# One sum in memory for all experts in place of an even and an odd one, in a two-layer hybrid backbone with a mixture of experts

## The chip, the cores and the metric

The kernel runs on one core of a Trainium2 chip, in one launch. The metric is the device time of that core in microseconds (us). Lower is better.

## What is computed

The reference is a two-layer backbone over 256 latent tokens and 256 context tokens of width 1024 (float32). Each layer has a mixer (state-space, gated-recurrence and delta-rule head groups) and then a mixture of 64 experts, of which every token uses 8. The change is in the second part:

```python
def _routed_experts(h, router_w, router_bias, w_gate, w_up, w_down):
    scores = jax.nn.sigmoid(h @ router_w)
    _, idx = lax.top_k(scores + router_bias, TOP_K)
    gate = ...
    ...
    def expert_block(args):
        xb, e = args
        return (jax.nn.silu(xb @ w_gate[e]) * (xb @ w_up[e])) @ w_down[e]
    ...
    return jnp.zeros_like(h).at[token].add(contrib)

def _moe(...):
    ...
    return routed + shared
...
h = h + g_f * _moe(...)
```

Layer 0 routes 512 tokens (4096 pairs of token and expert), layer 1 only the 256 latent tokens (2048 pairs). A shared expert, which every token uses, is added.

## The kernel before

Each engine (matrix, vector or DVE, scalar or ACT, Pool, and SP, which issues plain transfers) has its own instruction stream, written by hand, and they meet at semaphores. `S[name]` is a semaphore; `wait(name, n, l)` waits for its n-th count in layer `l`. A DMA adds 16 to its semaphore when it has landed.

After the mixer the token rows are stored to the array `ffn_rows` in memory, each with its 64 gates behind it. For each expert the list of its tokens (`idx_in`) comes out of a small matmul. An expert has one block of up to 128 rows; where it has at most 64 tokens all work is done on 64 ("narrow"), else on 128 ("wide"). The flag for this is `more`, which each engine loads from on-chip memory and branches on (`by_count` on Pool, L740 to L748). Rows of the list past the expert's last token point outside the array and are skipped.

The loop over experts runs in four slots `s` (expert e = 4i + s). Its work by engine:

- SP loads the 3 MB of weights of an expert (L531, L532 gate and up, L536 down), up to four experts ahead, as slots come free.
- Pool issues for expert e first `gather` for e+3 (L737: rows of `ffn_rows` into `xg[s]`, which stands in `featT` or `R`), once the matrix engine has read the slot; then it waits for both halves of expert e's scaled result (`oe_act`, `oe_dve`, L759 to L761) and for an earlier scatter (L763 to L765), and issues the scatter of e (L768): each row of `oe[s % 2]` is added to its token's row in memory by the DMA itself (`compute_op=ALU.add`). `pool_step` holds this.
- The matrix engine's step of e (`pe_step`) is: turn e's hidden values; gate and up projection of e+1 (128x256 matmuls); transpose the gathered rows of e+2 (L1743, waiting for the gather); down projection of e (128x512 matmuls).
- DVE and ACT scale half of e's result each with the token's gate into `oe[s % 2]` (L1665, L1056). Before that they wait for the scatter of e-2, which read the same buffer (L1658, L1051).

There are two sums in memory. Scatters of even experts add to `acc_dram` (`ffn_sum_even`), which is first filled with the shared expert's output (L551). Those of odd experts add to `acc_odd` (`ffn_sum_odd`), which SP fills with zeros from the tile `zero` during the input projections (L503 to L505). Two scatters that add to one array must not be in flight together, since both may touch the same token's row. So a scatter waits for the one of e-2, the last on its array.

After the last scatter SP reads both sums back (L601, L602) into `yraw` (which is `featT`) and `sums` (in `R`), and DVE does for each live tile of 128 tokens: add the two, multiply by the gate of the residual, add to `h` (L1711 to L1715). The live tiles are four in layer 0 and two in layer 1.

Of the kernel before, what the change touches and what calls it, by code (L numbers as in the profile page):

```python
# [8 lines left out]
F32 = mybir.dt.float32  # L9
I32 = mybir.dt.int32  # L10
U32 = mybir.dt.uint32
BF16 = mybir.dt.bfloat16
ALU = mybir.AluOpType
# [3 lines left out]
P = 128  # L17
DEPTH = 2
DM = 1024
# [130 lines left out]
def build(nc, A, out, scratch):  # L150
    f_dram, acc_dram, acc_odd = scratch
    with ExitStack() as ctx:
# [187 lines left out]
        for name, n in (  # L340
# [28 lines left out]
            ("sh_ps", 2), ("sh_silu", 1), ("sh_mul", 1), ("shd_ps", NT), ("shd_sb", NT), ("acc_zeroed", 16 * NT),  # L369
# [4 lines left out]
            ("sums_loaded", 32), ("gf_ps", 1),  # L374
# [12 lines left out]
        def tk(c):  # L387
            return slice(c * P, (c + 1) * P)
# [20 lines left out]
        def _(sp):  # L409
# [77 lines left out]
            for l in range(DEPTH):  # L487
# [15 lines left out]
                for c in live:  # L503
                    sp.dma_start(acc_odd[tk(c), :].rearrange("p (a b) -> p a b", b=32),
                                 zero[:, :].unsqueeze(1).to_broadcast([P, DM // 32, 32])).then_inc(S["acc_zeroed"], 16)  # L505
# [95 lines left out]
                sp.dma_start(yraw[:, rows, :], acc_odd.rearrange("(c p) f -> p c f", p=P)[:, rows]).then_inc(S["sums_loaded"], 16)  # L601
# [10 lines left out]
        def _(pool):  # L612
            G = nc.gpsimd

            def wait(name, n, l):
                pool.wait_ge(S[name], l * PER[name] + n)
                pool.sem_inc(S["past"], 1)
# [35 lines left out]
            for l in range(DEPTH):  # L653
# [96 lines left out]
                def pool_step(i, s, ahead):  # L750
# [12 lines left out]
                    if not (first and s < 2):  # L763
                        pool.wait_ge(S[f"scattered{s % 2}"], l * (8 * NE) + i * 32 + (s // 2) * 16)
                        pool.sem_inc(S["past"], 1)  # L765

                    def rows(n):
                        pool.indirect_dma_start((acc_dram, acc_odd)[s % 2], bass.IndirectOffsetOnAxis(idxS[s][0:n, 0:1].bitcast(U32), 0),  # L768
                                                oe[s % 2][0:n, :], None, bounds_check=TOK - 1, oob_is_err=False,
                                                compute_op=ALU.add).then_inc(S[f"scattered{s % 2}"], 16)  # L770
# [5 lines left out]
                wait("acc_zeroed", 16 * nl, l)  # L776
# [313 lines left out]
        def _(dve):  # L1090
# [92 lines left out]
            for l in range(DEPTH):  # L1183
# [527 lines left out]
                wait("sums_loaded", 16 + 32, l)  # L1711
                for c in live:
                    tt(sums[:, c, :], sums[:, c, :], yraw[:, c, :], ALU.add)
                    tt(sums[:, c, :], sums[:, c, :], bank(2 * (c // 2), 2), ALU.mult)
                    tt(h[:, c, :], h[:, c, :], sums[:, c, :], ALU.add)  # L1715
# [620 lines left out]
```

## Time and profile before

| what | us |
|---|---|
| median of 3 runs | 2808.56 |
| the runs | 2806.84 to 2814.77 |
| the profiled execution, its own time | 2818.87 |
| span of its trace | 2817.2 |
| matrix engine busy | 2371.4 (84%) |
| DVE busy | 1365.4 (48%) |
| ACT busy | 730.4 (26%) |
| Pool busy | 608.4 (22%) |

The profile is of one execution. Busy is the time in which an engine had an instruction running; transfers are told by queue: q1 is that of the plain transfers of SP, q0 that of the gathers and scatters of Pool. The experts' loop of layer 0 stands in the trace from 865 to 1524 us, that of layer 1 from 2207 to 2783 us. In the timeline an issue row such as `POOL L768 DMA_INDIRECT` lasts as long as Pool takes to write the transfer's list, not until the data have landed.

### The profile page before, as it was taken

To read this page: it belongs to the slowest core of one execution; us is meant where nothing else is said; L and a number is where in the kernel's file an instruction comes from. 1 tells how busy PE (TensorE), PEld (TensorE's weight loads), DVE (VectorE), ACT (ScalarE), POOL (GpSimd) and SP (SyncE) were. 2 spreads that over 40 slices of the span, in tenths; PEclk is the share of its full clock that TensorE was granted. 3 is DMA by queue.
4 is the path that set the end of the run, shared out by engine and by line. 5 is a ranking of instruction groups with operands and counts; after the bars stand their busy time and mean duration, and the time that the engine had idled before them with its cause. 6 is when DMAs were issued, how large, how long until landed. Compare 5 with 4: busy or idle time off the path is not lost.

```text
span 2817.2 us, 47122 instructions
## 1 busy us (share of the span) xinstructions
PE 2371.4 (84%) x15388; PEld 1547.9 (55%) x15389; DVE 1365.4 (48%) x2960; ACT 730.4 (26%) x1274; POOL 608.4 (22%) x640
## 2 busy tenths in 40 slices
PE   5999888886788989898996698888877888888884
PEld 2347788885644545454553245788866444444442
DVE  4433487875334444444432543367853444444443
ACT  2116333231112222222221114533221222222221
POOL 0000354450002222222221000135320122222221
PEclk9999899997889999999998799999989999999887
DMA  6643100001538999999995252200017899999993
GB/s 259 246 172 77 18 2 1 1 1 39 207 120 313 369 361 348 347 352 333 362 328 172 94 204 70 54 1 1 1 35 273 318 366 369 375 357 362 366 364 116
DMA packets 187925, 574.33 MB, mean 204 GB/s; under 512 B 55742, under 2 KB 99078, under 8 KB 148870
## 3 DMA queue, kind: packets, MB, share of 16 engines
q1 hardware_dynamic: 162950, 520.48, 49.9%
q0 software_dynamic: 24832, 51.97, 7.9%
q8 instruction: 86, 1.41, 0.2%
q14 instruction: 57, 0.47, 0.1%
HBM read 554.89 MB, written 53.15 MB: 216 GB/s over the span
## 4 chain that ended last, share of the span: by engine, by line
PE 52%; DMA 17%; DVE 14%; issue 6%; ACT 4%; DVEq 3%; POOLq 2%; ACTq 1%; SPq 0%; POOL 0%
PE ps L1739 47%; DMA featT<-ffn_rows,idx_in 11%; PE ps L1743 5%; DVE R L1102 3%; DMA R<-ffn_rows,idx_in 3%; DMA R<-in_exp_up 2%; ACT R L832 2%; DVEq L1099 2%; DVE featT L1102 2%; POOLq L744 1%; DVE R L1665 1%; DVE ring L1102 1%; DVE R L1376 1%; ACT L832 1%; DMA R<-ffn_sum_even 1%
## 5 line engine op out<-in xcount | busy, mean ns | idle before, releaser
L1739 PE MATMUL ps<-R 128*64 128x256 f32 (+6 forms) x9312 | 1263.7, 393 | 81.5 <-issue 25.3
L1739 PEld LDWEIGHTS ps<-R 128*64 128x64 f32 (+2 forms) x9312 | 752.2, 156 | 456.8 <-issue 236.5
L832 ACT ACTIVATE R<-ps 128x256 f32<-128x256 f32 (+3 forms) x395 | 175.5, 444 | 984.2 <-PE ps L1739 926.4
L1739 PE MATMUL ps<-featT,ring 128*128 128x512 f32 (+1 forms) x768 | 318.9, 573 | 0.3 <-issue 0.3
L1102 DVE TENSOR_TENSOR R<-R,ps 128x256 f32<-128x256 f32 (+2 forms) x250 | 143.7, 575 | 361.2 <-ACT R L832 232.3
L1665 DVE TENSOR_SCALAR R<-ps,idx_out 64x512 f32<-64x512 f32 x256 | 193.2, 755 | 170.7 <-PE ps L1739 168.8
L1739 PE MATMUL ps<-ring,R 128*128 128x128 f32 (+2 forms) x1200 | 243.9, 335 | 17.2 <-DVE ring L1102 8.4
L1111 DVE COPY R<-ps 128x512 f32<-128x512 f32 (+2 forms) x280 | 153.8, 549 | 212.6 <-PE ps L1743 181.0
L1056 ACT ACTIVATE R<-ps,idx_out 64x512 f32<-64x512 f32 x256 | 174.6, 682 | 280.6 <-PE ps L1739 279.0
L1739 PEld LDWEIGHTS ps<-featT,ring 128*128 128x128 f32 x768 | 150.6, 200 | 164.4 <-issue 158.5
L1743 PE MATMUL ps<-ident,featT 128*128 128x128 f32 x864 | 134.4, 306 | 126.5 <-DMA featT<-ffn_rows,idx_in 91.6
L1739 PEld LDWEIGHTS ps<-ring,R 128*128 128x128 f32 x1200 | 193.7, 198 | 49.5 <-issue 29.9
L669 POOL TENSOR_TENSOR R<-ring,lev 128x512 f32<-128x512 f32 x56 | 72.6, 1297 | 623.2 <-DVEq L1338 307.1
L768 POOL DMA_INDIRECT ffn_sum_even<-R,idx_out x64 | 94.9, 1483 | 495.6 <-DVE idx_in L1102 361.0
L1743 PEld LDWEIGHTS ps<-ident,featT 128*128 128x128 f32 x864 | 106.1, 155 | 169.8 <-DMA featT<-ffn_rows,idx_in 112.4
L768 POOL DMA_INDIRECT ffn_sum_odd<-R,idx_out x64 | 95.9, 1498 | 424.1 <-issue 290.1
L1036 ACT ACTIVATE R<-ps 128x512 f32<-128x512 f32 x128 | 76.6, 599 | 278.0 <-PE ps L1743 275.2
L737 POOL DMA_INDIRECT featT<-ffn_rows,idx_in x96 | 95.1, 990 | 245.1 <-issue 245.1
L1743 PE MATMUL ps<-ident,R 128*128 128x128 f32 x616 | 106.3, 290 | 26.0 <-DMA R<-ffn_rows,idx_in 23.7
L1739 PE MATMUL ps<-ring,featT 128*128 128x256 f32 x512 | 113.8, 383 | 1.0 <-issue 1.0
L1739 PEld LDWEIGHTS ps<-ring,featT 128*128 128x128 f32 x512 | 97.8, 192 | 17.1 <-issue 4.0
L669 POOL TENSOR_TENSOR R<-R,lev 128x512 f32<-128x512 f32 x56 | 72.9, 1302 | 116.5 <-PE ps L1739 89.1
(201 smaller groups left out, 1981.0 us busy)
## 6 DMA issues: line engine op xcount, KB each, us to landing
R<-in_exp_gate SPq DMA_DIRECT2D x128, 1024.0 KB
R<-in_exp_up SPq DMA_DIRECT2D x128, 1024.0 KB
R<-in_exp_down SPq DMA_DIRECT2D x128, 1024.0 KB
R<-in_w_mod SPq DMA_DIRECT2D x48, 1024.0 KB, 7.5
ring<-in_w_in SPq DMA_DIRECT2D x30, 1024.0 KB, 5.3
ring<-in_w_out SPq DMA_DIRECT2D x8, 1024.0 KB, 7.2
ffn_sum_odd<-zero SPq DMA_DIRECT2D x6, 512.0 KB, 11.0
ffn_rows<-X SPq DMA_DIRECT2D x6, 512.0 KB, 9.1
```

Of the source, the lines that this page charges most:

```text
L669: do(G.tensor_tensor(NTm[:, run % 2, :, :], AT[u % 2][:, :, :], lev[:, UNITS[u][1], j, :].unsqueeze(1).to_broadcast([P, HH, P]), ALU.mult) ...
L737: pool.indirect_dma_start(xg[s][0:n, :], None, f_dram, bass.IndirectOffsetOnAxis(idxG[s][0:n, 0:1].bitcast(U32), 0), bounds_check=TOK - 1, ...
L768: pool.indirect_dma_start((acc_dram, acc_odd)[s % 2], bass.IndirectOffsetOnAxis(idxS[s][0:n, 0:1].bitcast(U32), 0), oe[s % 2][0:n, :], Non ...
L832: do(C.activation(out_, in_, func, **kw), name)
L1036: do(C.activation(xgT[b][:, 0:4, :].rearrange("p k t -> p (k t)"), ps[:, 0, :], ACT.Identity), "xt_sb")
L1056: ins = C.activation(oe[s % 2][at_, 0:512], ps[0:HD, 4 + 2 * (s % 2) + u, :], ACT.Identity, scale=idxS[s][at_, 1:2])
L1099: dve.drain()
L1102: do(V.tensor_tensor(out_, a, b, op), name)
L1111: do(V.tensor_copy(out_, in_), name)
L1665: ins = V.tensor_scalar(oe[s % 2][at_, 512:DM], ps[HD:P, 4 + 2 * (s % 2) + u, :], idxS[s][at_, 1:2], None, ALU.mult)
L1739: return MM(out_, lhsT, rhs, start=start, stop=stop)
L1743: return nc.tensor.transpose(out_, in_, ident[0:k, 0:k])
```

## The change

One array `acc_dram` (`ffn_sum`) takes the scatters of all experts. It is filled with the shared expert's output as before; the array of zeros, its stores and its semaphore are gone. The scatter of e now waits for that of e-1: in slot s for the semaphore of the other parity, with the count that it has when e-1 has landed. Only the very first scatter waits for none. After the loop one array is read back, and DVE's addition of the two sums is gone. The two buffers `oe` and the waits of DVE and ACT for e-2 are as before.

```diff
--- before.py
+++ after.py
@@ -148,7 +148,7 @@
 
 
 def build(nc, A, out, scratch):
-    f_dram, acc_dram, acc_odd = scratch
+    f_dram, acc_dram = scratch
     with ExitStack() as ctx:
         def sb(name, shape, dt=F32):
             return ctx.enter_context(nc.sbuf_tensor(name, shape, dt))
@@ -366,12 +366,12 @@
             ("mask_ready", 1), ("pos_ps", 1), ("w_ready", 1), ("w_stored", 16),
             ("hot_ready", NE + 1), ("slot_ps", NSLOT), ("flag_ready", 1),
 
-            ("sh_ps", 2), ("sh_silu", 1), ("sh_mul", 1), ("shd_ps", NT), ("shd_sb", NT), ("acc_zeroed", 16 * NT),
+            ("sh_ps", 2), ("sh_silu", 1), ("sh_mul", 1), ("shd_ps", NT), ("shd_sb", NT), 
 
             ("w0", 0), ("w1", 0), ("w2", 0), ("w3", 0), ("wd0", 0), ("wd1", 0), ("wd2", 0), ("wd3", 0),
             ("gathered0", 4 * NE), ("gathered1", 4 * NE), ("gathered2", 4 * NE), ("gathered3", 4 * NE), ("xt_ps", NE), ("xt_sb", 2 * NE), ("gu_ps", NE), ("gu_silu", NE), ("gu_mul", NE), ("ht_ps", NE), ("ht_sb", NE),
             ("dn_ps", NE), ("oe_act", NE), ("oe_dve", NE), ("idx_in", NE), ("idx_out", NE), ("scattered0", 8 * NE), ("scattered1", 8 * NE),
-            ("sums_loaded", 32), ("gf_ps", 1),
+            ("sums_loaded", 16), ("gf_ps", 1),
 
             ("ov_w", 48 * OVER), ("ov_hot", OVER), ("ov_ip", OVER), ("ov_tab", OVER), ("ov_g", OVER), ("ov_xt", OVER), ("ov_xs", OVER),
             ("ov_gu", OVER), ("ov_sl", OVER), ("ov_mu", OVER), ("ov_dn", OVER),
@@ -500,9 +500,6 @@
                     if kind == "mod" and q < n_mod:
                         mod_block(at_mod + q)
                         q += 1
-                for c in live:
-                    sp.dma_start(acc_odd[tk(c), :].rearrange("p (a b) -> p a b", b=32),
-                                 zero[:, :].unsqueeze(1).to_broadcast([P, DM // 32, 32])).then_inc(S["acc_zeroed"], 16)
                 sp.dma_start(rw[:, :, :], A["router_w"][L1].rearrange("o (k p) n -> p (o k) n", p=P)).then_inc(S["rw_loaded"], 16)
                 wout = A["w_out"][L1].rearrange("o (k p) n -> p (o k) n", p=P)
 
@@ -598,7 +595,6 @@
                 for b in range(2):
                     wait(f"scattered{b}", 8 * NE, l)
                 rows = slice(live[0], NT)
-                sp.dma_start(yraw[:, rows, :], acc_odd.rearrange("(c p) f -> p c f", p=P)[:, rows]).then_inc(S["sums_loaded"], 16)
                 sp.dma_start(sums[:, rows, :], acc_dram.rearrange("(c p) f -> p c f", p=P)[:, rows]).then_inc(S["sums_loaded"], 16)
             sp.wait_ge(S["h_ready"], DEPTH + 1)
             sp.dma_start(grow[:, 0, :], A["norm_final"].rearrange("(o f) -> o f", o=1).to_broadcast([P, DM])).then_inc(S["head_loaded"], 16)
@@ -760,12 +756,13 @@
                     pool.wait_ge(S["oe_dve"], e + 1)
                     pool.sem_inc(S["past"], 1)
 
-                    if not (first and s < 2):
-                        pool.wait_ge(S[f"scattered{s % 2}"], l * (8 * NE) + i * 32 + (s // 2) * 16)
+
+                    if not (first and s == 0):
+                        pool.wait_ge(S[f"scattered{(s + 1) % 2}"], l * (8 * NE) + i * 32 + ((s + 1) // 2) * 16)
                         pool.sem_inc(S["past"], 1)
 
                     def rows(n):
-                        pool.indirect_dma_start((acc_dram, acc_odd)[s % 2], bass.IndirectOffsetOnAxis(idxS[s][0:n, 0:1].bitcast(U32), 0),
+                        pool.indirect_dma_start(acc_dram, bass.IndirectOffsetOnAxis(idxS[s][0:n, 0:1].bitcast(U32), 0),
                                                 oe[s % 2][0:n, :], None, bounds_check=TOK - 1, oob_is_err=False,
                                                 compute_op=ALU.add).then_inc(S[f"scattered{s % 2}"], 16)
                     by_count(i * NSLOT + s, rows)
@@ -773,7 +770,6 @@
                 for s in range(3):
                     gather(s, s)
 
-                wait("acc_zeroed", 16 * nl, l)
                 for b in range(2):
                     wait(f"x_stored{b}", 16 * nl, l)
                 for s in range(NSLOT):
@@ -1708,9 +1704,8 @@
                         dve.sem_inc(S[name], OVER)
 
                 wait("gf_ps", 1, l)
-                wait("sums_loaded", 16 + 32, l)
+                wait("sums_loaded", 16 + 16, l)
                 for c in live:
-                    tt(sums[:, c, :], sums[:, c, :], yraw[:, c, :], ALU.add)
                     tt(sums[:, c, :], sums[:, c, :], bank(2 * (c // 2), 2), ALU.mult)
                     tt(h[:, c, :], h[:, c, :], sums[:, c, :], ALU.add)
                 dve.drain().then_inc(S["h_ready"], 1)
@@ -2328,8 +2323,7 @@
         A[name] = nc.dram_tensor(f"in_{name}", a.shape, mybir.dt.from_np(a.dtype), kind="ExternalInput").ap()
     out = nc.dram_tensor("out", (1, SEQ, DM), F32, kind="ExternalOutput").ap()
     scratch = (nc.dram_tensor("ffn_rows", (TOK, FROW), F32, kind="Internal").ap(),
-               nc.dram_tensor("ffn_sum_even", (TOK, DM), F32, kind="Internal").ap(),
-               nc.dram_tensor("ffn_sum_odd", (TOK, DM), F32, kind="Internal").ap())
+               nc.dram_tensor("ffn_sum", (TOK, DM), F32, kind="Internal").ap())
     build(nc, A, out, scratch)
     r = run_bass_kernel_spmd(nc, [arrays], core_ids=[0])
     return r.results[0]["out"]
```

The order of Pool, slots 0 and 1 of the loop over experts 4 to 59 (`ffn_sum_even` and `ffn_sum_odd` are the two sums; the two DMA rows of one scatter are its wide and its narrow form). Before:

```order
L759 REGISTER_ALU
L764 REGISTER_ALU [waits oe_act,oe_dve]
L744 ISA [waits scattered0]
L744 TENSOR_LOAD more
...
L768 DMA ffn_sum_even<-R,idx_out 512x1024
...
L734 REGISTER_ALU [waits xt_ps]
L744 ISA [waits idx_in]
...
L737 DMA featT<-ffn_rows,idx_in 64x1088
...
L744 ISA [waits oe_act,oe_dve,scattered1]
...
L768 DMA ffn_sum_odd<-R,idx_out 512x1024
```

And with the change:

```order
L755 REGISTER_ALU
L761 REGISTER_ALU [waits oe_act,oe_dve]
L740 ISA [waits scattered1]
L740 TENSOR_LOAD more
...
L765 DMA ffn_sum<-R,idx_out 512x1024
...
L730 REGISTER_ALU [waits xt_ps]
L740 ISA [waits idx_in]
...
L733 DMA featT<-ffn_rows,idx_in 64x1088
...
L761 REGISTER_ALU [waits oe_act,oe_dve]
L740 ISA [waits scattered0]
...
L765 DMA ffn_sum<-R,idx_out 512x1024
```

The scatter of slot 0 waits for the semaphore of the odd scatters, that of slot 1 for that of the even ones, which is the scatter issued directly before it. The gather between them keeps its place.

The order of DVE after the loop of layer 0 (first tile and the beginning of the second; `R` holds the sum, `featT` the odd sum, `ps` the gate). Before:

```order
L1102 TENSOR_TENSOR R<-R,featT 128x1024 [waits sums_loaded,gf_ps]
L1102 TENSOR_TENSOR R<-R,ps 128x1024
L1102 TENSOR_TENSOR h<-h,R 128x1024
L1102 TENSOR_TENSOR R<-R,featT 128x1024
L1102 TENSOR_TENSOR R<-R,ps 128x1024
```

And with the change:

```order
L1098 TENSOR_TENSOR R<-R,ps 128x1024 [waits sums_loaded,gf_ps]
L1098 TENSOR_TENSOR h<-h,R 128x1024
L1098 TENSOR_TENSOR R<-R,ps 128x1024
```

One of three passes a tile is gone.

## Rows read from the trace of the kernel before

**Rows 1.** The page: the chain that ended last, its share of the span by line.

```profile
PE ps L1739 47%; DMA featT<-ffn_rows,idx_in 11%; PE ps L1743 5%; DVE R L1102 3%; DMA R<-ffn_rows,idx_in 3%; DMA R<-in_exp_up 2%; ACT R L832 2%; DVEq L1099 2%; DVE featT L1102 2%; POOLq L744 1%; DVE R L1665 1%; DVE ring L1102 1%; DVE R L1376
```

**Rows 2.** Windows: us, busy (instructions) by engine, matrix clock, DMA share, GB/s.

```profile
864.70:1524.00 659.30, 597.69 (x4436) 325.23 (x4432) 267.18 (x608) 146.34 (x249) 156.61 (x124) 0.96 0.96 334
2206.90:2783.00 576.10, 491.37 (x3392) 260.61 (x3388) 252.18 (x607) 146.59 (x250) 149.84 (x124) 0.93 0.97 350
269.00:290.00 21.00, 20.74 (x93) 17.26 (x92) 4.01 (x10) 10.72 (x11) 0.00 (x0) 1.00 0.91 149
```

**Rows 3.** Waits in the loops: us in total, times, longest; layer 1, then 0.

```profile
PE ps L1743 <- DMA featT<-ffn_rows,idx_in: 58.7, 25, 4.8
...
PE ps L1743 <- DMA featT<-ffn_rows,idx_in: 32.9, 14, 5.7
```

**Rows 4.** Timeline, Pool: start, us, instruction [idle before]; each loop's first, five between.

```profile
864.66 1.52 POOL L768 DMA_INDIRECT ffn_sum_even<-R,idx_out  x1 [19.15 <-DVE idx_in L1102]
...
2206.89 1.49 POOL L768 DMA_INDIRECT ffn_sum_even<-R,idx_out  x1 [13.69 <-DVE idx_in L1102]
...
2355.46 1.44 POOL L768 DMA_INDIRECT ffn_sum_even<-R,idx_out  x1 [6.85 <-DVE idx_in L1102]
2357.20 0.97 POOL L737 DMA_INDIRECT featT<-ffn_rows,idx_in  x1 [0.30 <-issue]
2362.68 1.44 POOL L768 DMA_INDIRECT ffn_sum_odd<-R,idx_out  x1 [4.51 <-DVE idx_in L1102]
...
2373.61 1.44 POOL L768 DMA_INDIRECT ffn_sum_even<-R,idx_out  x1 [8.21 <-DVE idx_in L1102]
...
2380.38 1.44 POOL L768 DMA_INDIRECT ffn_sum_odd<-R,idx_out  x1 [4.07 <-issue]
```

**Rows 5.** Chain that ended last: start, us, what; from 2357 us.

```profile
2357.20 8.56 DMA featT<-ffn_rows,idx_in
...
2415.19 29.84 DMA R<-in_exp_up
```

**Rows 6.** Last scatters: chain (layer 0 and 1), and timeline of the last in layer 1.

```profile
1523.96 6.09 DMA ffn_sum_odd<-R,idx_out
...
2782.96 4.48 DMA ffn_sum_odd<-R,idx_out
...
2779.79 1.52 DVE L1665 TENSOR_SCALAR R<-ps,idx_out 64x512 f32<-64x512 f32 x2 [4.99 <-PE ps L1739]
```

**Rows 7.** DMA, q0 (packets, MB, share) in 2437.68:2442.2, 2442.2:2443.6, 1388:1391.5.

```profile
q0 software_dynamic: 29, 0.03, 2.4%
q0 software_dynamic: 54, 0.08, 29.3%
...
q0 software_dynamic: 70, 0.21, 27.3%
```

**Rows 8.** Groups by form: down projections of layer 0's loop, then layer 1's.

```profile
L1739 PE MATMUL ps<-R 128*64 128x512 f32 x744 | 187.0, 639 | 4.5 <-DVE R L1111 2.7 <-issue 1.2
...
L1739 PE MATMUL ps<-R 128*64 128x512 f32 x552 | 153.9, 688 | 6.6 <-issue 5.5
```

**Rows 9.** Read-back: timeline (layer 0), chain (layer 1), issues to landing (2048, 1024 KB).

```profile
1532.15 0.39 SPq L601 DMA_DIRECT2D featT<-ffn_sum_odd  x1
...
1545.97 1.23 DVE L1102 TENSOR_TENSOR R<-R,featT 128x1024 f32<-128x1024 f32 x1 [23.55 <-DMA R<-ffn_sum_even]
1547.27 1.22 DVE L1102 TENSOR_TENSOR R<-R,ps 128x1024 f32<-128x1024 f32 x1
...
2789.95 7.00 DMA R<-ffn_sum_even
...
featT<-ffn_sum_odd SPq DMA_DIRECT2D x1, 2048.0 KB, 8.2
...
featT<-ffn_sum_odd SPq DMA_DIRECT2D x1, 1024.0 KB, 4.9
```

**Rows 10.** Timeline, SP: the zero stores of layer 0.

```profile
268.96 15.05 SPq L504 DMA_DIRECT2D ffn_sum_odd<-zero  x4
```

## The prediction

> **What bounds the kernel now.** I read the chain that ended last on the page first [rows 1]: matmuls of one line hold 47% of it, but 11% + 3% are gathers of token rows and 2% are loads of weights. So inside the expert loops a transfer and not arithmetic decides part of the time. The windows of the two loops say how much [rows 2]: 659.3 us for the 64 experts of layer 0 and 576.1 us for layer 1, together 44% of the span. In both the DMA engines are busy (share 0.96 and 0.97), and in layer 1 the matrix engine is busy 491 of 576 us only. The waits name the cause [rows 3]: in layer 1 it sat 58.7 us before transposes (L1743) whose rows came from a gather, in layer 0 32.9 us (and less before those of the slot in `R`).
>
> The timeline of the Pool engine shows why a gather can be late [rows 4]. Pool does everything in one order: scatter of expert e-1, gather for e+3, scatter of e, gather for e+4. A gather is issued 1.74 us after the scatter in front of it (2355.46 and 2357.20), and in the chain it lands 8.56 us later at 2365.76, where the transposes begin [rows 5]. Those are in the matrix engine's step of expert e+1; after them come its down projection, the scaling (L1056, L1665), and the scatter of e+1 at 2373.61. So each second scatter is tied to the one two before it through a gather, and the gaps alternate: 7.2, 10.9, 6.8 us between the four issues shown. Two such ties, of odd and of even experts, run side by side.
>
> **The change, part by part.**
>
> *The wait (slower).* In the order of Pool [the two extracts of Pool's loop in the section on the change] scatter e waited for scatter e-2; now it waits for e-1. Before, that wait was never late: with gaps of 7 to 11 us two of them give 17 us or more. What is queued behind it on Pool is the gather for e+4, and behind that the matrix engine. So the price depends on how long a scatter takes to land, which the trace tells only at the loops' ends, where no weights move: 6.09 us and 4.48 us [rows 6]. Under load I bound it from the DMA queue of Pool. The scatter issued at 2437.68 is followed by 4.5 us in which its queue moves 0.03 MB, then by 1.4 us with 0.08 MB (its rows), then come the bytes of the gather behind it [rows 7]: its data are over 5.9 us after the issue, and the semaphore comes later still. From above, the gather queued behind a scatter lands 1.74 + 8.56 = 10.3 us after that scatter's issue [rows 4, 5]. I take 7.6 us for an expert of up to 64 rows, nearer to the row of the thing itself. For an expert with more rows ("wide") the queue after the issue at 1381.75 is still moving 0.21 MB between 6.25 and 9.75 us [rows 7]; I take 9.9 us. From the landing to the next issue Pool needs the semaphore wait, a value load and a branch; the same path after the scaling takes from 2779.79 + 1.52 = 2781.31 to 2782.96, 1.65 us, say 1.7 [rows 6].
>
> That gives each gap a floor: 9.3 us, and 11.6 us behind a wide expert. The number of wide experts comes from the down projections: 8 matmuls an expert, 16 a wide one, so 744 = 512 + 8 x 29 and 552 = 512 + 8 x 5 [rows 8]; 28 of the 29 have a successor. The floors of the 63 gaps of layer 0 add up to 35 x 9.3 + 28 x 11.6 = 650 us, of layer 1 to 58 x 9.3 + 5 x 11.6 = 597 us. The gaps themselves add up to 659.3 us (864.66 to 1523.96) and 576.1 us (2206.89 to 2782.96) [rows 4, 6]. The floors are only an average, and a gap that is longer for another reason gives nothing back. Laid over the 126 gaps between the 128 issue rows (first and last of each loop in rows 4 and 6), 30 gaps of layer 0 and 36 of layer 1 lie under their floor, by 56 and 80 us in total. How much of this is lost? A short gap that is stretched delays one tie; the long gap behind it is held by the other tie, whose gather was issued before, so it shrinks by as much until the two together reach two floors. I therefore take gaps in pairs, and count only what two floors exceed the measured pair: 22.6 us in layer 0, 35.3 us in layer 1. Sum **+58 us**. Both ends: with 7.0 and 9.2 us for the landing the pairs give 9.8 + 15.8 = +26 us, with 8.0 and 10.3 us 35.1 + 52.0 = +87 us. The slope is steep: half a microsecond of landing time is worth about 30 us.
>
> *One read-back in place of two (faster).* In layer 0 the first of two 2 MB reads is issued at 1532.15, the second behind it, and DVE starts at 1545.97, released by the second; the first alone landed 8.2 us after its issue. With one read left DVE starts at about 1532.15 + 8.2 + 0.1 = 1540.4: -5.5 us. In layer 1 the second is issued at 2789.95 and lands at 2796.95; the first, issued 0.4 us earlier, landed after 4.9, at 2794.4: -2.6 us [rows 9]. All of it lies on the chain.
>
> *The additions (faster).* DVE does three passes for each live tile (sum of the halves, gate, residual), 1.30 us from start to start [rows 9]; the first falls away (the extract of DVE's rows in the section on the change). Four tiles in layer 0 are -5.2 us, two in layer 1 -2.6 us, on the chain, since the passes follow each other without a gap and the next layer starts from their result.
>
> *Zeroing (nothing).* Six stores of zeros go. The four of layer 0 keep the sync queue for 15.05 us from 268.96 on and the DMA engines at 0.91, but the matrix engine is busy 20.74 of those 21.0 us, and the queue has only the router weights behind it before a long wait [rows 2, 10]. They cover nothing and hide under the matmuls.
>
> Sum: +58 - 5.5 - 2.6 - 5.2 - 2.6 = **+42 us**. The profiled execution took 2818.87 us (span 2817.2), 10 us over the median of 2808.56; I put the difference on the median: 2808.6 + 42 = 2851 us.
>
> The trace has the first bytes of a scatter 4.5 us after its issue under load [rows 7], and 4.48 us even for a whole one without load. The Trainium skill, page "DMA: Bandwidth & Descriptors", section "Anatomy of one DMA — SWDGE (gpsimd) path", gives a DMA issued by GpSimd about 2.0 us plus its bytes at 436 GB/s, which for 64 rows of 4 KB would be an estimated 2.6 us. By that the wait would cost nothing, and the sum would be the -16 us of the other terms; the trace does not agree.
>
> **The rivals.**
>
> *The landing is covered (faster).* If a scatter, now alone on its array and never beside another scatter, lands as at the loops' ends (4.5 to 6.1 us), the floor is 6.2 to 7.8 us, under nearly every gap (the shortest is 6.0), and the pairs lose under 1 us. Then only the savings remain: 2808.6 - 16 = 2793 us. It decides from a landing under about 6.5 us. For: rows 6. Against: rows 7, where the queue is shared with the weights in every loop step, since DMA is busy 96%. The skill's rule above would also end here. Chance 0.07.
>
> *The weights hold the loop (no change).* The chain has stretches of 29.84 us in which a weight load and not a gather is waited for [rows 5], and layer 1 moves 350 GB/s. If the weights set the pace, a late scatter is absorbed wherever they are late too, and only the floors' own excess remains: nothing in layer 0 and 597 - 576 = 21 us in layer 1, so 2808.6 + 21 - 16 = 2814 us, inside 0.3%. Against: most pieces of layer 1's chain are gathers. Chance 0.09.
>
> *Nothing is absorbed (much slower).* If both ties are tight, each stretched gap is lost in full: 56 + 80 = 136 us, 2808.6 + 136 - 16 = 2929 us. Against: the long gap has a matrix-engine wait in it (58.7 us in 25 waits, 2.3 us each [rows 3]), which can shrink. Chance 0.08.
>
> *The wait does not hold Pool* (its count is reached already, so the change is the read-back alone) would look like the first rival; the counts in the two extracts speak against it. It is in that chance.
>
> **How the numbers follow.** The forecast, loops slower by 26 to 87 us and the ends faster by 16, has the other 0.76: 2819 to 2880 us, likeliest 2851. The range goes somewhat beyond on both sides, half way into "nothing is absorbed" and to the edge of "weights hold the loop": 2814 to 2892. About 0.3%, 8 us, is what a measurement of this kernel can tell from no change. Slower: all of the forecast but its lowest edge and the third rival, 0.83. Same: the second rival and that edge, 0.10. Faster: 0.07.
>
> **What would show it.** In the changed profile: the gaps between scatter issues hardly under 9 us and no longer alternating; loops of about 682 and 611 us; Pool idle before a scatter until the DMA of the one in front; DVE's first pass starting some 8 us after the read is issued in layer 0; two passes a tile. It is wrong if gaps of 7 us survive (the landing is short) or if loop times stay while the gaps level out (everything absorbed).

## The result, and the profile after

The changed kernel takes 2858.53 us (median of 4 runs, 2845.71 to 2861.67) against 2808.95 us (4 runs) for the kernel before: ratio 1.0165, 95% interval 1.013 to 1.0199. It is slower by 49.6 us in the medians, by 37 to 56 us within the interval; 42 us and 2851 us were forecast, with a range of 2814 to 2892 us. The profiled execution took 2861.67 us (span 2859.9), 42.7 us over the span of before.

The page has the chain that ended last by line. It answers to [rows 1]:

```profile
PE 43%; DMA 27%; DVE 14%; issue 6%; ACT 3%; POOLq 3%; DVEq 2%; ACTq 1%; POOL 0%; SPq 0%
PE ps L1734 40%; DMA ffn_sum<-R,idx_out 19%; DMA featT<-ffn_rows,idx_in 5%; PE ps L1738 3%; DVE R L1098 3%; ACT R L828 2%; POOLq L740 2%; DMA R<-ffn_rows,idx_in 2%; DVE featT L1098 2%; DVEq L1095 1%; DVE ring L1098 1%; DVE R L1372 1%; ACT L
```

A scatter's landing was hardly in the chain before; now it holds 19% of the span, and the gathers fell from 14% to 7%. The windows of the two loops, first scatter to last, in the columns of [rows 2]:

```profile
864.50:1561.60 697.10, 613.77 (x4438) 330.42 (x4434) 267.25 (x608) 146.14 (x249) 156.00 (x124) 0.94 0.92 316
2230.40:2831.40 601.00, 499.16 (x3395) 263.55 (x3392) 251.30 (x607) 147.39 (x250) 150.01 (x124) 0.92 0.94 336
```

Layer 0's loop grew from 659.3 to 697.1 us, layer 1's from 576.1 to 600.9 us, together by 62.7 us, and the DMA engines are less busy (0.92 and 0.94 against 0.96 and 0.97). The rest went the other way: between the loops 682.9 us became 668.8, and after the last scatter 34.2 became 28.5. That is -19.8 us, and with -0.1 before the first scatter the sum is the 42.7 us.

The waits of the matrix engine for gathers in the stretches of layer 0 and layer 1, as in [rows 3] (us in total, times, longest):

```profile
PE ps L1738 <- DMA featT<-ffn_rows,idx_in: 57.3, 22, 6.8
PE ps L1738 <- DMA R<-ffn_rows,idx_in: 17.6, 6, 5.9
...
PE ps L1738 <- DMA featT<-ffn_rows,idx_in: 74.7, 32, 6.2
PE ps L1738 <- DMA R<-ffn_rows,idx_in: 14.1, 10, 3.9
```

They rose from 52.7 to 74.9 us in layer 0 and from 62.6 to 88.8 us in layer 1. The matrix engine was also busy for longer with the same instructions: in layer 0 613.77 us at a mean granted clock of 0.94, where it had been 597.69 us at 0.96, and in layer 1 499.16 us at 0.92, where it had been 491.37 us at 0.93 [rows 2]. The timeline of Pool in layer 1, near the place of [rows 4]:

```profile
2380.57 1.44 POOL L765 DMA_INDIRECT ffn_sum<-R,idx_out  x1 [7.04 <-issue]
2382.53 0.96 POOL L733 DMA_INDIRECT R<-ffn_rows,idx_in  x1 [0.53 <-issue]
2391.03 1.44 POOL L765 DMA_INDIRECT ffn_sum<-R,idx_out  x1 [7.54 <-issue]
...
2401.11 1.44 POOL L765 DMA_INDIRECT ffn_sum<-R,idx_out  x1 [7.37 <-issue]
...
2410.34 1.44 POOL L765 DMA_INDIRECT ffn_sum<-R,idx_out  x1 [6.52 <-issue]
```

These are the 16th to the 19th scatter of the layer, and the gaps are 10.5, 10.1 and 9.2 us. In the kernel before the same three gaps were 9.8, 7.2 and 10.9 us (the four issues of [rows 4] are the 17th to the 20th). The short gap grew by 2.9 us, and the long one behind it shrank by 1.7 us only. The chain in the same stretch shows what sets them (start, us, what):

```profile
2380.57 8.79 DMA ffn_sum<-R,idx_out
2389.53 0.29 POOLq L740
2389.86 0.15 POOLq L740
...
2391.03 8.41 DMA ffn_sum<-R,idx_out
...
2401.11 7.57 DMA ffn_sum<-R,idx_out
```

A scatter lands after 8.79 us, Pool loads the flag and branches, and 1.67 us after the landing the next scatter leaves. That repeats without a matmul in between. In layer 0 the chain changes between the two kinds of cause:

```profile
1125.51 11.80 DMA ffn_sum<-R,idx_out
...
1138.87 10.37 DMA ffn_sum<-R,idx_out
...
1150.91 7.60 DMA ffn_sum<-R,idx_out
...
1162.03 11.50 DMA R<-ffn_rows,idx_in
1173.57 1.97 PE ps L1738 x8
```

Three landings in a row, then a gather that was queued behind the scatter of 1160.01 and holds the transposes at 1173.57. The ends, from the chain, answer to [rows 6] and [rows 9]:

```profile
1561.60 5.91 DMA ffn_sum<-R,idx_out
...
1569.60 7.72 DMA R<-ffn_sum
1577.42 1.22 DVE R L1098
1578.71 1.22 DVE h L1098
1580.01 1.22 DVE R L1098
...
2831.35 4.41 DMA ffn_sum<-R,idx_out
...
2837.82 4.78 DMA R<-ffn_sum
2842.69 1.22 DVE R L1098
```

One read of 2 MB holds DVE for 7.8 us, where two held it for 13.8; two passes a tile are left.

### The profile page after: what moved, and what is told of

The parts are those of the page before. It is cut to its first block, busy times and chain, and to the rows that moved or that the text cites. A ratio compares the mean times of both kernels' runs of the same rounds, so it can differ in the third digit from the quotient of the medians.

```text
span 2859.9 us, 47130 instructions
## 1 busy us (share of the span) xinstructions
PE 2388.9 (84%) x15388; PEld 1551.0 (54%) x15389; DVE 1353.7 (47%) x2954; ACT 729.6 (26%) x1274; POOL 607.7 (21%) x640
## 4 chain that ended last, share of the span: by engine, by line
PE 43%; DMA 27%; DVE 14%; issue 6%; ACT 3%; POOLq 3%; DVEq 2%; ACTq 1%; POOL 0%; SPq 0%
PE ps L1734 40%; DMA ffn_sum<-R,idx_out 19%; DMA featT<-ffn_rows,idx_in 5%; PE ps L1738 3%; DVE R L1098 3%; ACT R L828 2%; POOLq L740 2%; DMA R<-ffn_rows,idx_in 2%; DVE featT L1098 2%; DVEq L1095 1%; DVE ring L1098 1%; DVE R L1372 1%; ACT L828 1%; DMA ring<-in_sh_down 1%; DVE R L1661 1%
## 5 line engine op out<-in xcount | busy, mean ns | idle before, releaser
L1734 PE MATMUL ps<-R 128*64 128x256 f32 (+6 forms) x9312 | 1278.9, 397 | 72.8 <-DVEq L1377 19.2
L765 POOL DMA_INDIRECT ffn_sum<-R,idx_out x128 | 190.6, 1489 | 983.5 <-issue 796.1
L1734 PE MATMUL ps<-featT,ring 128*128 128x512 f32 (+1 forms) x768 | 313.1, 564 | 0.3 <-issue 0.3
L1738 PE MATMUL ps<-ident,featT 128*128 128x128 f32 x864 | 141.6, 317 | 165.8 <-DMA featT<-ffn_rows,idx_in 131.9
L1738 PEld LDWEIGHTS ps<-ident,featT 128*128 128x128 f32 x864 | 111.9, 161 | 210.0 <-DMA featT<-ffn_rows,idx_in 158.5
L1738 PEld LDWEIGHTS ps<-ident,R 128*128 128x128 f32 x616 | 67.0, 145 | 55.9 <-DMA R<-ffn_rows,idx_in 39.5
## 6 DMA issues: line engine op xcount, KB each, us to landing
R<-in_exp_up SPq DMA_DIRECT2D x128, 1024.0 KB, 10.4
```

What stands on the lines that cost most here:

```text
L765: pool.indirect_dma_start(acc_dram, bass.IndirectOffsetOnAxis(idxS[s][0:n, 0:1].bitcast(U32), 0), oe[s % 2][0:n, :], None, bounds_check=TO ...
L1734: return MM(out_, lhsT, rhs, start=start, stop=stop)
L1738: return nc.tensor.transpose(out_, in_, ident[0:k, 0:k])
```

## The experiments

The theory to be tested is that the whole loss is the new wait, which sets a floor under each gap between scatters (landing plus 1.7 us) and also holds the gather that stands behind the scatter in Pool's order. The rivals in what follows are that one array is dearer by itself, that the loss is the floor alone or the gather alone, and that the weights hold the loop.

"Loops" below are the times from the first to the last of a layer's 64 scatter issues in the profiled execution. "Landing" is the mean over these 64, from the issue to the last of the scatter's semaphore counts in the trace. (In the trace of the kernel before, 34 of the 128 scatters lack some of their 16 counts; the last one recorded stands for them.) Both are of one execution each. Ratios are to the kernel before on the same chip, with their 95% interval; its own medians beside the experiments were 2812.7 us (e1 to e4), 2812.0 us (e5 to e8), 2810.2 us (e9 to e11) and 2813.7 us (e12).

| kernel | median, us | ratio | loops, us | landing, us |
|---|---|---|---|---|
| before | 2808.95 | 1 | 659.3, 576.1 | 8.9, 7.8 |
| the change | 2858.53 | 1.0165 (1.013 to 1.0199) | 697.1, 600.9 | 8.1, 7.5 |
| e1 the wait alone | 2875.9 | 1.0223 (1.0191 to 1.0254) | 693.6, 601.4 | 8.0, 7.5 |
| e2 the ends alone | 2793.73 | 0.9937 (0.9919 to 0.9955) | 658.5, 573.8 | 8.8, 7.8 |
| e3 before, early gather | 2804.44 | 0.9965 (0.9947 to 0.9984) | 648.1, 575.2 | 9.0, 7.9 |
| e4 change, early gather | 2810.79 | 0.9991 (0.9977 to 1.0005) | 662.2, 590.1 | 8.8, 7.7 |
| e5 before, less traffic | 2775.05 | 0.9867 (0.9852 to 0.9882) | 632.4, 562.0 | 7.4, 7.4 |
| e6 change, less traffic | 2789.19 | 0.9915 (0.9896 to 0.9933) | 663.4, 559.1 | 7.3, 6.7 |
| e7 change, zero stores kept | 2850.04 | 1.0124 (1.0105 to 1.0143) | 683.6, 606.4 | 8.2, 7.5 |
| e8 two sums, early gather and read | 2802.36 | 0.9965 (0.9952 to 0.9979) | 647.6, 575.8 | 9.2, 7.9 |
| e9 change, swapped | 2804.88 | 0.9985 (0.9972 to 0.9998) | 658.9, 579.0 | 8.8, 7.5 |
| e10 before, swapped | 2789.85 | 0.9932 (0.9915 to 0.9948) | 646.6, 567.2 | 9.7, 8.1 |
| e11 change, early, less traffic | 2669.08 | 0.9515 (0.9471 to 0.9559) | 598.5, 508.3 | 7.6, 6.3 |
| e12 before, early, less traffic | 2620.98 | 0.9314 (0.9295 to 0.9332) | 587.6, 459.0 | 8.0, 7.6 |

**The wait alone.** Kernel before, with

```diff
-                    if not (first and s < 2):
-                        pool.wait_ge(S[f"scattered{s % 2}"], l * (8 * NE) + i * 32 + (s // 2) * 16)
+                    if not (first and s == 0):
+                        pool.wait_ge(S[f"scattered{(s + 1) % 2}"], l * (8 * NE) + i * 32 + ((s + 1) // 2) * 16)
```

> The kernel before with both sums, zero stores, read-backs and additions kept; only the wait of each scatter is changed from the one of e-2 to the one of e-1. Theory (the wait costs the loops, the ends give back): both loops as long as in the changed kernel, 63 gaps of about 697 us in layer 0 and 601 us in layer 1, together 55 to 65 us more than before, stretches outside the loops as before; time about 2809 + 62 = 2871 us. Rival (one array in place of two is dearer by itself, because every scatter now adds to rows that the one in front of it has just written): the loops grow by under 20 us here, time under 2830 us.

Measured: 2875.9 us, +63 us on the median of before beside it (2812.7). The loops took 693.6 and 601.4 us, +59.6 us, as in the changed kernel within 4 us. One array instead of two adds nothing that can be seen; the rival falls.

**The ends alone.** The zero stores, the read of the odd sum and the addition taken out of the kernel before:

```diff
-                sp.dma_start(yraw[:, rows, :], acc_odd.rearrange("(c p) f -> p c f", p=P)[:, rows]).then_inc(S["sums_loaded"], 16)
...
-                    tt(sums[:, c, :], sums[:, c, :], yraw[:, c, :], ALU.add)
```

> The kernel before without the zero stores, the read-back of the odd sum and DVE's addition; what the odd experts contribute is left out of the result. Waits of the scatters as before. Theory: loops as before (659 and 576 us for the 63 gaps), ends shorter by 10.7 us after layer 0 and 5.2 us after layer 1, time about 2809 - 16 = 2793 us; if the changed kernel's 14 us between the loops are all of this part, 2789 us. Rival (the ends are hidden or given back by a later start of something else): within 5 us of before.

Measured: 2793.73 us, -0.63%, which is -18 us. This version leaves the odd experts out of the result, and layer 1 has six wide experts by it where there were five. The loops stayed (-0.8 and -2.3 us). Between the loops it was 669.1 us (-13.8), at the end 28.6 us (-5.6). The two halves add up: a ratio of 1.0223 and one of 0.9937 make 1.0159, against 1.0165 measured for both together.

**The gather out of the way.** Pool's step issues the gather of e+4 where it issued that of e+3, one expert earlier, so that it stands in front of the wait and not behind it:

```diff
-                    if ahead > 3:
-                        if not (first and s == 0):
-                            pool.wait_ge(S["xt_ps"], e)
-                            pool.sem_inc(S["past"], 1)
-                        gather((s + 3) % NSLOT, i * NSLOT + s + 3)
+                    if ahead > 4:
+                        pool.wait_ge(S["xt_ps"], e + 1)
+                        pool.sem_inc(S["past"], 1)
+                        gather(s, i * NSLOT + s + 4)
...
-                for s in range(3):
+                for s in range(4):
                     gather(s, s)
```

> The kernel before with Pool's order changed: the gather of expert e+4 is issued before the scatter of e and not behind it, as soon as the matrix engine has turned e's rows and the list of e+4 is there; a fourth gather is issued before the loop. Two sums and the wait for e-2 stay. Theory (scatters are tied two by two through a gather queued behind them): the matrix engine's waits for gathers (120 us in both loops) nearly vanish, and the loops fall to what matmuls or weights allow: layer 0 about 600 to 620 us, layer 1 about 550 to 570 us, time 2750 to 2775 us. Rival (the gathers are late because the DMA engines are full): the gather only lands as late as before, loops within 10 us of before, time above 2795 us.

> The changed kernel with the same early gather. Theory (with the wait for e-1 each gap has a floor of landing + 1.7 us, whatever the gather does): the loops stay at the sum of the floors, about 660 to 690 us and 590 to 600 us, so the time falls by 5 to 40 us only, to 2820 to 2850 us, and Pool waits for the scatter in front before nearly every scatter. Rival (the wait costs only because it holds the gather behind it): with the gather in front of it the cost vanishes, the loops come within 15 us of those of the kernel before with the early gather, time under 2790 us.

Both gave part of an answer. In e3 the matrix engine's waits for gathers vanished, as the theory said (no such row is left in either loop), but the time fell by 8 us only, outside what it forecast. The waits of layer 0 and layer 1 and the chain say where it went:

```profile
PE ps L1738 <- issue: 47.3, 24, 6.4
...
PE ps L1738 <- issue: 85.3, 44, 6.1
...
2313.01 28.53 DMA R<-in_exp_up
2341.54 1.21 issue
2342.75 3.70 PE ps L1738 x32
```

The matrix engine now stops before the gate and up projection, and the chain runs through a load of up weights that takes 28.5 us from its issue. The kernel before was close to this second bound: layer 1's loop did not get shorter at all (575.2 against 576.1 us). In layer 1's loop loads of up weights hold 30% of e3's chain, in layer 0's 20%. So in layer 1 gathers that came late by 63 us in total cost nearly nothing, because the weights were as late. The rival of e3 was right on the time, and not in its reason: the gathers take as long to land as before (9.5 and 7.9 us on the mean, after 9.6 and 8.0), but they come in time.

In e4 the cost of the wait is then what a floor costs. The chain through it:

```profile
1218.75 7.09 DMA ffn_sum<-R,idx_out
...
1227.53 8.46 DMA ffn_sum<-R,idx_out
...
1237.59 10.01 DMA ffn_sum<-R,idx_out
...
1249.20 10.36 DMA ffn_sum<-R,idx_out
```

All 126 gaps of e4 are the landing plus 1.45 to 1.71 us: the loops are the floor itself. They are 14.1 and 14.9 us longer than in e3, 29 us together. The time came out at 2811 us, under the 2820 us that the theory set as its lower edge and far above the rival's 2790. Against the changed kernel the loops are 35 and 11 us shorter. So of the wait's 62.7 us 29 us are the floor. The gather held behind it takes 45.7 us, less the 12.1 us that the same place of the gather had cost in the kernel before (659.3 - 648.1 and 576.1 - 575.2), which is 34 us. These are differences of single executions; e7 below shows by how much such loops differ.

**The same without a head start.** In e4 the gather also left earlier. Here gather and scatter only change places behind the scaling:

```diff
                     pool.wait_ge(S["oe_act"], e + 1)
                     pool.wait_ge(S["oe_dve"], e + 1)
                     pool.sem_inc(S["past"], 1)
+                    if ahead > 4:
+                        pool.wait_ge(S["xt_ps"], e + 1)
+                        pool.sem_inc(S["past"], 1)
+                        gather(s, i * NSLOT + s + 4)
```

and the gather of e+3 at the head of the step is gone.

> The changed kernel with gather and scatter swapped behind the scaling: once expert e is scaled, Pool issues the gather of e+4 first, and only then waits for the scatter of e-1 and issues the scatter of e. The gather so starts at the point where it would in a loop without the new wait, no earlier than the scaling as in e4. Theory (of the 62 us that the wait costs, the larger part is the gather held behind it, and 29 us are the floor of landing plus restart): loops near those of e4 (662 and 590 us), at most 10 us longer each, time 2808 to 2828 us. Rival (e4 was faster because its gathers start some 5 us ahead of the scaling, not because they are out of the wait): loops near those of the changed kernel (690 to 697 and 595 to 601 us), time above 2840 us.

> The same swap in the kernel before, with its two sums and the wait for e-2: the partner of e9. Theory (before the change nothing late stands in front of the gather, so the swap only starts it 1.7 us earlier): between the kernel before and e3, 2800 to 2812 us, loops 650 to 659 us and 575 us. Then e9 is slower than this one by the floor alone: 29 us in the loops, 10 to 15 us in the time. Rival (scatters that leave 1.3 us later cost by themselves): slower than before.

Measured: e9 2804.88 us, under the range expected, with loops of 658.9 and 579.0 us. So the order alone does it, and the rival falls: the changed kernel with its two issues swapped is no slower than the kernel before. Here too each of the 126 gaps is the landing plus 1.45 to 1.71 us. e10 took 2789.85 us, 10 us under the lower edge of what was expected, and is the fastest of the versions that compute the whole result: -0.68% against the kernel before (0.9915 to 0.9948), -2.3% against the changed one (0.9932 over 1.0165). Its waits for gathers, in layer 0 and in layer 1:

```profile
PE ps L1742 <- DMA featT<-ffn_rows,idx_in: 0.8, 1, 0.8
...
PE ps L1742 <- DMA featT<-ffn_rows,idx_in: 2.6, 4, 1.2
```

The gather leaves only 1.7 us sooner than in the kernel before, but its packets now stand in front of the scatter's in Pool's queue: its mean landing fell from 9.6 to 7.9 us (layer 0) and from 8.0 to 7.0 us (layer 1), and the scatter's rose from 8.9 to 9.7 and from 7.8 to 8.1 us. That longer landing is now waited for at times: before it fills `oe` again DVE waited for a scatter 16 times in the two loops, 29.9 us in total and at most 4.0 us, which it never did in the kernel before. In e9 the same swap did not bring the gather's landing forward: the gather's mean landing is 8.96 and 7.25 us, where it was 8.53 and 7.45 us in the changed kernel. There the gain is that the gather no longer stands behind the wait. e9 against e10 is again the floor alone: 12.3 + 11.8 = 24 us in the loops and 15 us in the time. By this pair the swap gave 60.1 us in the changed kernel's loops and 21.6 us in those of the kernel before, so the held gather is 38.5 us of the 62.7, where e3 and e4 have 34. Why e9 and e10 are faster than e4 and e3 was not settled.

**Less traffic.** The down weights are loaded for the first four experts of a layer only; the right ones of the other 60 are left out, in all four of these kernels:

```diff
                     sp.wait_ge(S["dn_ps"], l * NE + i * NSLOT + (s - NSLOT + 1))
                     past()
-                    down_of(s, i * NSLOT + s)
+                    sp.sem_inc(S[f"wd{s}"], 16)
```

> The kernel before with the down weights loaded for the first four experts of a layer only (later experts reuse them, so a third of the weight traffic and the right weights of 60 experts are left out). It is the partner of the next run. Theory (the landing of a scatter is long because its packets share the DMA engines with the weights): the landing falls from 8.9 and 7.8 us on the mean of the two loops to under 7.5 and 6.5 us, the gathers land sooner too, and the loops fall to about 590 to 630 us and 480 to 530 us, where the matmuls bound them. Rival (landing is a fixed cost of Pool's queue): landings stay within 0.5 us of before.

> The changed kernel with the same third of the weight traffic left out. Theory (landing is traffic): the wait for the scatter in front costs the loops under 25 us against the partner run, where it cost 62 us with full traffic, and after the savings of 16 to 20 us at the ends the two are within 10 us of each other. Rival (landing is fixed at 7.5 to 9 us): each gap keeps its floor of 9.3 us or more while the partner's gaps shrink, so the loops are longer by 100 us or more.

In e5 the landing fell to 7.4 us in layer 0, as expected, but in layer 1 from 7.8 only to 7.4 us, where under 6.5 was expected; in layer 1 it so stayed within the rival's 0.5 us. Layer 1's loop took 562 us, not 530: its waits for gathers are 72.5 us (62.6 before), so a third of the weights' bytes made little difference while the gathers held it. In e6 the wait cost 31.0 us in layer 0 and -2.9 us in layer 1, 28 us where under 25 was expected and 62.7 with full traffic, and the time was 14 us over the partner's instead of within 10. The rival (100 us) is far off. The weight traffic is so a part of the landing, and this third of it not the larger part: 6.4 us for a narrow expert remain in both layers of e6.

> The changed kernel with the early gather of e4 and without the down weights of 60 experts a layer, as in e5 and e6. Theory (the gather behind the wait is what is left of the cost in e6, since landings of 6.4 and 8.5 us put the floors at 8.1 and 10.2 us): the loops fall under those of e5, to 590 to 632 us and 510 to 560 us, time under 2760 us. Rival (the floor is what is left): the loops stay at 655 us and more in layer 0, time above 2780 us.

> The kernel before with the early gather of e3 and without the down weights of 60 experts a layer: the partner of e11. Theory (with the gather out of the way the wait costs only where a gap lies under landing plus restart): e11's loops took 598.5 and 508.3 us, bound by the landing in 116 of 126 gaps; here they fall to what matmuls and the remaining weights allow, 580 to 595 us and 470 to 500 us, so loops 20 to 40 us shorter than in e11 and, with the ends 16 to 20 us dearer, a time 0 to 25 us under e11's 2669 us. Rival (the landing did not bound e11, the matmuls did): loops within 8 us of e11's, time 8 to 20 us above 2669 us.

e11 fell by 120 us against e6, to 2669 us (under 2760 was expected), with 116 of its 126 gaps at the floor. Its theory took this for the price of the gather behind the wait, and e12 shows that it is not. e12 came to 2621 us, 48 us under e11 (0 to 25 were expected): loops shorter than in e11 by 10.9 and 49.3 us, 60 us in all, more than the 20 to 40 expected; the rival falls. The early gather took 115.7 us off the loops with the wait (e6 to e11) and 147.8 us without it (e5 to e12). What it removes under light traffic is the tie of gather and scatter that the kernel before has too; the wait itself costs more once it is gone, 60 us and not 28. The chain of e12 holds 2% of transfers:

```profile
PE 73%; DVE 14%; ACT 4%; issue 3%; DMA 2%; DVEq 2%; ACTq 1%; POOLq 1%; POOL 0%; SPq 0%
```

The matmuls allow a gap of 7.3 us in layer 1 (459.0 over 63), and the landing with its restart holds it at 8.1 (508.3 over 63). Of the 49.3 us 15 are not idle time: the matrix engine was busy 467.22 us in e11, at a granted clock of 0.97, and 452.23 us in e12, at 1.00 (columns as in [rows 2], layer 1 of e11 and of e12):

```profile
2131.10:2639.40 508.30, 467.22 (x3392) 250.46 (x3388) 251.43 (x607) 146.81 (x250) 149.82 (x123) 0.97 0.80 273
...
2130.10:2589.10 459.00, 452.23 (x3392) 247.28 (x3388) 251.51 (x607) 146.45 (x250) 151.10 (x122) 1.00 0.88 302
```

So the same wait costs 63 us in one surrounding, 29 in another, 28 in the third and 60 in the fourth.

**The zero stores.** The changed kernel with the six stores of zeros to a spare array kept.

> The changed kernel with the six stores of zeros put back, to an array that nothing reads. Theory (they hide under the input projections): within 0.3% of the changed kernel, 2850 to 2867 us. Rival (they delay the loads of the projections' weights): slower by 5 us or more in the stretch before the first loop, and again before the second, above 2868 us.

Measured: 2850.04 us, the lower edge of what was expected, and 862.1 us to the first scatter against 864.5 without them. They hide. The run shows something else besides: loops of 683.6 and 606.4 us in a kernel whose loops have the same instructions as the changed one's (697.1 and 600.9). Of the 13.5 us in layer 0 9.6 are busy time of the matrix engine (604.18 us at a clock of 0.95, against 613.77 at 0.94). So these loops differ by 5 to 14 us between single executions; the split between the layers is no better known than that.

**A read-back before the end.** Two sums, the early gather of e3, and the even sum read as soon as its last scatter has landed:

```diff
                 with sp.If(none > 0):
                     sp.sem_inc(S["ov_w"], PER["ov_w"])
+                    sp.wait_ge(S["scattered0"], l * PER["scattered0"] + 8 * NE)
+                    sp.dma_start(yraw[:, rows, :], acc_dram.rearrange("(c p) f -> p c f", p=P)[:, rows]).then_inc(S["sums_loaded"], 16)
...
-                sp.dma_start(yraw[:, rows, :], acc_odd.rearrange("(c p) f -> p c f", p=P)[:, rows]).then_inc(S["sums_loaded"], 16)
-                sp.dma_start(sums[:, rows, :], acc_dram.rearrange("(c p) f -> p c f", p=P)[:, rows]).then_inc(S["sums_loaded"], 16)
+                sp.dma_start(sums[:, rows, :], acc_odd.rearrange("(c p) f -> p c f", p=P)[:, rows]).then_inc(S["sums_loaded"], 16)
```

> A version meant to beat both: the kernel before (two sums, wait for e-2) with the early gather of e3, and with the even sum read back as soon as the last even scatter has landed, some 7 us before the last odd one lands, so that one read of 2 MB is left behind the last scatter as in the changed kernel. Theory: the early gather gives 8 us, the earlier read 5.5 us in layer 0 and 2.6 us in layer 1, time about 2812 - 16 = 2796 us. Rival (the early read collides with the last odd scatter and delays its landing by what it saves): same as e3, 2804 us.

Measured: 2802.36 us, ratio 0.9965, the same as e3's. The chain has the reason:

```profile
1508.26 10.53 DMA ffn_sum_odd<-R,idx_out
...
1521.69 7.94 DMA R<-ffn_sum_odd
```

The last odd scatter lands after 10.53 us, where it took 6.09 [rows 6]: the early read was issued 0.4 us behind it and moves at the same time. In layer 1 it lands after 8.40 us, where it took 4.48. The read behind it is short (7.94 us), but 4.4 us of what it saves are paid there. Between the loops it is 680.4 us (679.5 in e3), after the last scatter 36.7 us (34.3 in e3). The rival holds.

## Why the prediction was right

*The mechanism.* It was right: the loops lose by the wait, the ends give back, and short gaps go. e1 and e2 show the two halves apart, +63 and -18 us, against +58 and -16 forecast. The sum of the loops was helped by luck, as told under *The absorption*.

*The floor.* The restart of 1.7 us is 1.67 us in the chain. The landings taken, 7.6 us narrow and 9.9 us wide, are in the trace of before 8.0 and 10.1 us in layer 0 and 7.7 and 9.7 us in layer 1 (without the last scatter of each loop); in the changed kernel they are 7.3 and 9.2, 7.4 and 9.5 us. The prediction took the landing as the same before and after. Its mean fell by 0.8 us in layer 0, while the DMA engines were less busy (0.92 after 0.96). By the prediction's own slope for layer 0 (25 us for one microsecond) that is worth some 20 us, which the loop does not show.

*The absorption.* The pairs were to lose 22.6 us in layer 0 and 35.3 in layer 1; it was 37.8 and 24.8 us, with e7 at 24.3 and 30.3 and e1 at 34.3 and 25.3. The sum was right (57.9 for 62.7, 54.6 and 59.6 us), but all three executions lie over the forecast in layer 0 and under it in layer 1: two errors of opposite sign, and that they cancel is luck. With the landings of the changed kernel's own trace put into the prediction's sum of pairs it gives 11.2 us in layer 0 and 27.5 in layer 1. So in layer 1, where 50 of the 63 gaps are at their floor, floor plus pairs was the right model, and in layer 0 it leaves out 26.6 of 37.8 us. There the sum of landing plus 1.7 us over the 63 gaps is 620 us, 77 us below the loop, and 33 gaps are held by the landing in front. These 33 are together 41.1 us longer than in the kernel before, and the other 30 only 3.3 us shorter: the long gaps gave almost nothing back. Ten of the 30 have a wait of the matrix engine for a gather in the step before them (35.8 us); in the other 20 it waited for no gather, and mostly its own step of 10.4 or 12.1 us between two down projections set the gap, so that such a gap had nothing to give back.

*A term that is missing.* Told by the matrix engine, layer 0's 37.8 us are 22.2 us more of waiting for gathers and 16.1 us more of being busy with the same instructions, at a granted clock of 0.94 after 0.96. The prediction has no term for the clock. In most of these runs a loop with more idle time of the matrix engine has a lower clock too (layer 1: 0.92 in the changed kernel, 1.00 in e12), but no experiment separates the two, and whether the new wait causes the lower clock stays open.

*The ends.* Layer 0's read gave 6.0 us (5.5 forecast), the last layer's end 5.7 us in all (5.2), the additions 5.2 and 2.6 us as forecast. Between the loops 14.1 us were won against 10.7. The 3.4 us more are within what single executions differ by: that stretch took 679.1 to 682.9 us in the six kernels with both reads at the end (before, e1, e3, e5, e10, e12) and 668.8 to 674.2 us in the seven with one (the change, e2, e4, e6, e7, e9, e11), and the two means are 10.2 us apart.

*Zeroing.* Nothing, as forecast (e7; the first scatter is at 860.0 to 867.2 us in the kernels with zero stores and at 860.0 to 864.5 us in those without).

*The page's rule.* The estimate of 2.6 us for a landing from the Trainium skill, page "DMA: Bandwidth & Descriptors", section "Anatomy of one DMA — SWDGE (gpsimd) path", is not what these loops show: the shortest mean of any loop here is 6.3 us, at two thirds of the weight traffic. By it the wait would have cost nothing.

*The rivals.* "The landing is covered" fell, as did "nothing is absorbed" (136 us). "The weights hold the loop" was nearer to the truth than its chance of 0.09 says: in the kernel before, e3 showed that layer 1 is as long with all its gathers in time. That bound hides the old waits for gathers, not the new one for landings, so the time was still not that rival's.

## What to carry to other kernels

A wait for an earlier transfer on an issuing engine can cost twice: it puts a floor of landing plus restart under the loop, and it holds whatever is queued behind it. Look at the second first; here it was 34 to 39 of 63 us, and swapping two issues gave 50 us back, more than the removed second sum had ever been worth (18 us). Measure it against the same swap without the wait, since part of such a gain (12 to 22 us here, and all of it under light traffic) belongs to the kernel as it was. And the price of such a floor is not a constant to be added: it is what the floor exceeds the loop's next bound, so it was 24 to 29 us beside the weights' bound and 60 us where that bound was lifted.

## What was not expected of the hardware

Of two transfers that Pool issued right behind each other in the kernel with two sums, the one in front landed sooner. With the gather in front of the scatter (e10) the gather's mean landing fell by 1.7 us in layer 0 and 1.0 us in layer 1, and the scatter's rose by 0.8 and 0.3 us, at the same bytes. Leaving out nearly a third of the weight traffic took 1.5 us off a landing of 8.9 us in layer 0, but only 0.4 us off 7.8 us in layer 1 (e5); in the changed kernel it took 0.8 us off both (e6).
